# Row indices read in place by the gathers, and an early square root ahead of the norms' squares, in a decoder layer with product-key experts

## The reference, cut to what matters

```python
def peer(x, w_q, sub_keys, u_tab, v_tab):        # 8 heads, 128 keys, top 16, 128*128 experts
    ...
        best, pos = lax.top_k(cand.reshape(TOKEN_BLOCK, PEER_HEADS, PEER_TOPK * PEER_TOPK), PEER_TOPK)
        ids = jnp.take_along_axis(cand_ids.reshape(...), pos, axis=-1)
        g = jax.nn.softmax(best, axis=-1)
        u = u_tab[ids]
        v = v_tab[ids]
        h = jax.nn.gelu(jnp.einsum('td,thkd->thk', xb, u))
        w = (g * h.astype(jnp.float32)).astype(xb.dtype)
        return jnp.einsum('thk,thkd->td', w, v)
x = layer_norm(ALPHA * x + mixed @ w_out[i], ln1_g[i], ln1_b[i])
x = layer_norm(ALPHA * x + peer(x, ...), ln2_g[i], ln2_b[i])
x = x + jax.nn.sigmoid(x @ w_pg + b_pg) * (p[i] @ W_p)
```

## Time and profile before

| | |
|---|---|
| median of 3 runs | 3905.25 us (3902.64 to 3909.58) |
| the profiled execution | 3903.89 us, its span 3902.1 us |
| PE busy | 3808.9 us (98% of the span) |
| PEld (weight loads) busy | 3471.3 us (89%) |
| DVE busy | 2682.2 us (69%) |
| ACT busy | 1403.7 us (36%) |
| POOL busy | 1265.6 us (32%) |
| mean DMA rate | 219 GB/s |
| granted TensorE clock, mean | 0.994 |

### The profile page before, as it was taken

The page is one execution under the profiler, slowest core; times in us unless marked ns, Lnnn a source line. Parts: engine busy times, 40 slices in busy tenths (PEclk is TensorE's granted clock), DMA queues, the critical chain, the costliest instruction groups (busy, mean ns, idle before and its releaser), DMA issues.

```text
span 3902.1 us, 57973 instructions
## 1 busy us (share of the span) xinstructions
PE 3808.9 (98%) x20449; PEld 3471.3 (89%) x20449; DVE 2682.2 (69%) x3814; ACT 1403.7 (36%) x1992; POOL 1265.6 (32%) x620
## 2 busy tenths in 40 slices
PE   8999999999998999999999999989999999999999
PEld 6888888878886889999999999989999999999777
DVE  3555555534413899878878878778888888898642
ACT  4433444441114223446546545222222222222442
POOL 4444444434443447422222222212212211222233
PEclk9999999999999999999999999999999999999999
DMA  4222222224433324698998898978877877787332
GB/s 156 95 97 97 102 94 94 94 99 152 148 121 108 108 89 160 232 367 321 361 373 314 340 378 328 404 294 315 306 288 279 318 289 283 285 311 278 119 105 78
DMA packets 210825, 856.40 MB, mean 219 GB/s; under 512 B 17520, under 2 KB 107824, under 8 KB 119216
## 3 DMA queue, kind: packets, MB, share of 16 engines
q1 hardware_dynamic: 137648, 515.62, 36.6%
q0 software_dynamic: 41600, 302.04, 19.2%
q10 hardware_dynamic: 31488, 37.76, 2.7%
HBM read 788.21 MB, written 67.11 MB: 219 GB/s over the span
## 4 chain that ended last, share of the span: by engine, by line
PE 75%; DVE 9%; DMA 7%; DVEq 3%; ACT 3%; issue 2%; ACTq 1%; SPq 0%
PE bank L631 24%; PE bank L633 23%; PE bank L632 23%; DMA raw<-ws 7%; DVE wlo L1611 2%; PE bank L875 2%; DVEq L1625 2%; DVE yacc L1715 2%; ACT whi L1027 1%; DVE sc L1416 1%; PE bank L674 1%; DVEq L1709 1%; PE bank L693 1%; DVE hot L1600 1%; DVE res L1757 1%
## 5 line engine op out<-in xcount | busy, mean ns | idle before, releaser
L1027 ACT ACTIVATE whi<-raw 128x1024 fp32r<-128x1024 f32 x784 | 820.6, 1057 | 2253.9 <-PE bank L633 1429.2
L631 PE MATMUL bank<-ahi,whi 128*128 128x352 f32 (+1 forms) x3968 | 1434.6, 362 | 32.2 <-DVE alo L1365 7.9
L632 PE MATMUL bank<-alo,whi 128*128 128x352 f32 (+1 forms) x3968 | 1413.8, 356 | 0.0
L633 PE MATMUL bank<-ahi,wlo 128*128 128x352 f32 (+1 forms) x3968 | 1413.6, 356 | 0.0
L594 POOL TENSOR_TENSOR wlo<-raw,whi 128x1024 fp32r<-128x1024 f32 x316 | 792.0, 2510 | 1050.3 <-ACT whi L1027 1021.5
L631 PEld LDWEIGHTS bank<-ahi,whi 128*128 128x128 f32 x3968 | 749.8, 189 | 126.7 <-issue 35.9
L633 PEld LDWEIGHTS bank<-ahi,wlo 128*128 128x128 f32 x3968 | 749.4, 189 | 77.3
L632 PEld LDWEIGHTS bank<-alo,whi 128*128 128x128 f32 x3968 | 749.5, 189 | 72.1 <-issue 0.5
L1611 DVE TENSOR_TENSOR wlo<-raw,whi 128x1024 fp32r<-128x1024 f32 x472 | 574.7, 1223 | 190.6 <-ACT whi L1027 188.3
L631 PE MATMUL bank<-xwhi,whi 128*128 128x384 f32 x2048 | 686.7, 335 | 19.3 <-ACT hst L1226 10.3
L633 PE MATMUL bank<-xwhi,wlo 128*128 128x384 f32 x2048 | 685.7, 335 | 0.0
(11 more groups left out here) (218 smaller groups left out, 2809.8 us busy)
## 6 DMA issues: line engine op xcount, KB each, us to landing
raw<-ws SPq DMA_DIRECT2D x394, 1024.0 KB, 4.9
gelu_spill<-hst ACTq DMA_DIRECT2D x128, 192.0 KB, 3.7
route_spill<-gst SPq DMA_DIRECT2D x24, 1024.0 KB, 14.8
hg<-gelu_spill SPq DMA_DIRECT2D x64, 384.0 KB, 6.7
hg<-route_spill SPq DMA_DIRECT2D x64, 384.0 KB, 7.4
gate_spill<-gout ACTq DMA_DIRECT2D x32, 256.0 KB, 2.1
gl<-gate_spill SPq DMA_DIRECT2D x32, 256.0 KB, 2.7
xin<-xT SPq DMA_DIRECT2D x8, 512.0 KB, 8.6
```

Source lines behind the costliest of these rows:

```text
L631: pe.matmul(ps_out, hi, xh, start=first, stop=False)
L632: pe.matmul(ps_out, hi, xl, start=False, stop=False)
L633: return pe.matmul(ps_out, lo, xh, start=False, stop=last)
L1027: act.activation(whi[:, s], raw[:, s // 2, s % 2], ACT.Copy).then_inc(hi_done, 1)
```

## The change

GpSimd reads each gather's index straight from `idx` or `xg`; `idxs`, `name_rows` and all its calls are gone, with the drains around the copies. The dots and additions themselves increment a new semaphore `rows_used`, for which GpSimd waits before it fills a buffer of the ring again. The first gather of `u_tab` waits for `idx_ok` (now incremented once, with the drain after the picks' transposes are copied) and for `xg_in`, for which VectorE waited before. The first gathers of `v_tab` wait on GpSimd for `blk_done` at `B6`. In `norm_squares` ScalarE first takes the square root of `eps` into one column of `std`.

```diff
-        idxs = small("idxs", [P, RING, 8], U32)
+        rows_used = sem("rows_used")
-            def gather_rows(first, n_rows, table, rows):
-
-                for n in range(n_rows):
-                    s = n % RING
-                    pool.wait_ge(idx_ok, first + n + 1)
+            def gather_u():
+
+                pool.wait_ge(idx_ok, 1)
+                pool.wait_ge(xg_in, 16 * NJ)
+                for n in range(NUP):
+                    if n >= RING:
+                        pool.wait_ge(rows_used, n - RING + 1)
+                    at_col = xg[:, 0, n:n + 1].bitcast(U32) if n < NXP else idx[:, n - NXP:n - NXP + 1]
                     nc.gpsimd.indirect_dma_start(
-                        rows[:, s], None, table,
-                        bass.IndirectOffsetOnAxis(ap=idxs[:, s, 0:1], axis=0)).then_inc(rows_in[s], 16)
+                        urows[:, n % RING], None, u_tab,
+                        bass.IndirectOffsetOnAxis(ap=at_col, axis=0)).then_inc(rows_in[n % RING], 16)
+
+            def gather_v():
+
+                pool.wait_ge(blk_done, B6)
+                for n in range(NP):
+                    if n >= RING:
+                        pool.wait_ge(rows_used, NUP + n - RING + 1)
+                    nc.gpsimd.indirect_dma_start(
+                        vrows[:, n % RING], None, v_tab,
+                        bass.IndirectOffsetOnAxis(ap=idx[:, n:n + 1], axis=0)).then_inc(rows_in[n % RING], 16)
...
             def norm_squares(i, n, src):
+
+                act.activation(std[:, 0:1], eps[:], ACT.Sqrt)
                 for k in range(n):
...
-            dve.drain()
+            dve.drain().then_inc(idx_ok, 1)
...
-            def name_rows(n, s, extra=False):
-
-                src = xg[:, 0, n:n + 1].bitcast(U32) if extra else idx[:, bass.ds(n, 1)]
-                dve.tensor_copy(idxs[:, s, 0:1], src).then_inc(idx_ok, 1)
-
-            def dot(n, m, s, more=True):
+            def dot(n, m, s):
...
                 dve.scalar_tensor_tensor(rows, rows, 1.0, x1n[:, :, TD:T], ALU.mult, ALU.mult,
-                                         accum_out=hd[:, bass.ds(n, 1)])
-                dve.drain()
-                if more:
-                    name_rows(n + RING, s)
+                                         accum_out=hd[:, bass.ds(n, 1)]).then_inc(rows_used, 1)
...
-            dve.wait_ge(xg_in, 16 * NJ)
-            for n in range(RING):
-                name_rows(n, n, extra=True)
             dve.wait_ge(x1e_ok, 5)
...
-                    dve.scalar_tensor_tensor(yacc[:], vrows[:, s], w, yacc[:], ALU.mult, ALU.add)
-                dve.drain()
-                if more:
-                    name_rows(n + RING, s)
+                    dve.scalar_tensor_tensor(yacc[:], vrows[:, s], w, yacc[:], ALU.mult, ALU.add
+                                             ).then_inc(rows_used, 1)
...
             dve.wait_ge(blk_done, B6)
-            for n in range(RING):
-                name_rows(n, n)
             dve.wait_ge(p_in, 16)
```

More of the change, by code:

```diff
@@ L607, in spread_picks @@
                                    ).then_inc(xg_in, 16)
[L609 to L616 removed]
+            def gather_u():
[5 more added lines that the diff above has]
+                    at_col = xg[:, 0, n:n + 1].bitcast(U32) if n < NXP else idx[:, n - NXP:n - NXP + 1]
+                    nc.gpsimd.indirect_dma_start(
+                        urows[:, n % RING], None, u_tab,
[8 more added lines that the diff above has]
+                        bass.IndirectOffsetOnAxis(ap=idx[:, n:n + 1], axis=0)).then_inc(rows_in[n % RING], 16)
             lo_parts(0, DVE_LO)
             spread_picks()
[L620 to L621 removed]
+            gather_u()
+            gather_v()
             pool.wait_ge(lo_done, B7)
@@ L1633, in extra_dot @@
                 dve.scalar_tensor_tensor(rows, rows, 1.0, x1e[:, :, TD:T], ALU.mult, ALU.mult,
-                                         accum_out=hx[:, n:n + 1])
-                dve.drain()
[L1636 to L1639, removed]
+                                         accum_out=hx[:, n:n + 1]).then_inc(rows_used, 1)
                 if n == NXP - 1:
@@ L1687, in _ @@
                 if with_dot:
-                    dot(n - NXP, n // RING, n % RING, more=n + RING < NUP)
+                    dot(n - NXP, n // RING, n % RING)
                     n += 1
@@ L1705, in expert_weights, with add_rows @@
                                   ).then_inc(w_ok, 1)
-            def add_rows(n, m, s, first=False, more=True):
+            def add_rows(n, m, s, first=False):
                 dve.drain()
@@ L1712, in add_rows @@
                 if first:
-                    dve.tensor_scalar(yacc[:], vrows[:, s], w, None, ALU.mult)
+                    dve.tensor_scalar(yacc[:], vrows[:, s], w, None, ALU.mult).then_inc(rows_used, 1)
                 else:
-                    dve.scalar_tensor_tensor(yacc[:], vrows[:, s], w, yacc[:], ALU.mult, ALU.add)
-                dve.drain()
-                if more:
-                    name_rows(n + RING, s)
+                    dve.scalar_tensor_tensor(yacc[:], vrows[:, s], w, yacc[:], ALU.mult, ALU.add
+                                             ).then_inc(rows_used, 1)
             for k in range(8):
@@ L1769, in add_values @@
                     else:
-                        add_rows(8 * g + u, 2 * g + u // RING, u % RING, more=not (last and u >= RING))
+                        add_rows(8 * g + u, 2 * g + u // RING, u % RING)
                     if ahead:
```

## The result

The changed kernel takes 3886.02 us (median of 5 runs, 3882.45 to 3886.93); the kernel before took 3904.87 beside it (5 runs, 3901.25 to 3909.58). The profiled executions' spans are 3902.1 and 3880.7 us.

A forecast was written before the change was run, and what follows sets the result against it. TensorE, with 75% of the chain, was taken as the bound, so only its idle time could shrink. Terms -3.8 - 0.2 + 3.5 - 2.8 + 1.35 = -1.95 us took 3905.25 to 3903.3, range 3893 to 3911.

The forecast's parts named there:

- Part 4: Value stage: without copy and drains after `add_rows`, five back edges shorten by 0.36 us each, a sixth wait by 1.0; -2.8.
- lower bound of -8.9: Value stage: the most that removing copies and drains after additions could give, TensorE's six waits for `res`, 8.9 us.
- Part 1: Routing tiles: without copy and drains after dots, 3.3 us less in looped first halves, 0.5 in second halves; -3.8 us.
- Rival A: Tiles and value stage: VectorE is the bound, so dots and adds count fully where TensorE idles; 3890 us, chance 0.2.
- Part 2: Ahead of the tiles' first `wlo`: four copies go and the wait for `xg_in` moves to GpSimd; -0.2 us.
- Part 3: Before the value stage: four first `v_tab` gathers go 12 us sooner and slow a weight load on the path; +3.5 us.
- promised sign: Before the value stage: early `v_tab` gathers make the weight load on the path land in 12 to 13 us, not 9.19.
- lower bound of 0: Before the value stage: early gathers cost nothing if the load's bytes are all ahead of theirs.
- Rival B: Before the value stage: early gathers halve the load from their issue and delay later loads; 3912 us, chance 0.12.
- Part 5: Three norms: the early square root of `eps` costs 1.45 us in the third, three removed loads give 0.1; +1.35 us.
- rival C: Norms: squares need another table load, 1.28 us more in the third and 0.3 in the second; 3904.9 us, chance 0.08.

The follow-up runs named there:

- 8 later: The kernel before with eight more drains on VectorE ahead of its value loop, copies kept: 3890.69 us, ratio 0.9965.
- v side alone: The kernel before with only the change on the side of `v_tab`; dots and norms as before: 3893.98 us, ratio 0.9982.
- u side alone: The kernel before with only the change on the side of `u_tab` (160 dots without copy and drains): 3880.54 us, ratio 0.9943.

## Why the prediction was wrong

**Part 4 failed at one step, and it was the largest: it took the time at the back edge for fixed.** The prediction had read 7.07 us without work behind `wlo`, called them the cost of jumping back, and only shortened the path by the copy's 0.36. An idle time that nothing in the rows explains was booked as a constant. In truth it hung on where the loop stands in the program, and any edit ahead of the loop that removes or adds instructions moves it. The shift by eight drains shows it: 12.5 us of value stage; the comparison with 1076.1 in place of 1079.6 makes it 9. The term that was worked out is worth nothing: with the loop in a good place, the value stage takes 1067.1 us with copies (8 later) and 1067.5 without (v side alone). TensorE's waits of 8.9 us were the right quantity to look at; I priced what stood beside their cause. The lower bound of -8.9 was nearly the size of the gain, by luck, since it stood for something else.

**Part 1 was right in first halves and failed in second ones.** It had priced 33 dots of the looped tiles at 0.10 us, since `wlo` behind a dot then waits for `whi` alone, and nothing in the unrolled tiles. The looped first halves got shorter by 0.9 us each, 2.7 in all where 3.3 was taken, and the last tile's by nothing. The period of a step with a dot is 4.83 us where it was 4.93, and 4.84 was promised:

```profile
2084.09 1.22 DVE L1626 TENSOR_TENSOR wlo<-raw,whi 128x1024 fp32r<-128x1024 f32 x1 [2.41 <-ACT whi L1040]
...
2088.92 1.23 DVE L1626 TENSOR_TENSOR wlo<-raw,whi 128x1024 fp32r<-128x1024 f32 x1 [0.19 <-ACT whi L1040]
```

The step "in second halves the transfers are full, and a request made 0.3 us earlier moves no byte sooner" is what failed: 0.5 us was taken, the second halves got shorter by 4.4, and their copies put back alone cost 7.7. The queue is full, but the request stands in a loop with the landing of the load before it (two buffers of `raw`), and what a late load costs is paid by the next tile's first one-hots. The trace of the kernel before had the sign: of the 2.4 us that TensorE idles from 2118 to 2185, none lies ahead of 2182, and one wait of 2.8 us for `hot2w` ends the stretch. Rival A had the size: it would be true, the prediction said, "if the tiles get shorter by 2 us each", and they got shorter by 9.5 / 5 = 1.9 each. But its mechanism did not come: `wlo` moved by 0.09 to 0.10 us in its period and no more. "VectorE is the bound" was too coarse; "VectorE is in the loads' loop" is what the traces point to.

**Part 2** (-0.2): the first one-hot matmul starts at 1616.63 before and 1616.66 after, and from 1614.3 to 1617.0 in all sixteen kernels; nothing to see.

**Part 3** (+3.5) was sized wrongly. GpSimd's timeline in the changed kernel has the first gather go out with the last expert block:

```profile
2550.95 1.14 POOL L627 DMA_INDIRECT vrows<-v_tab,idx  x1 [33.91 <-PE bank L646]
```

But the load that was to be slowed down had been issued earlier and landed 1 us behind it; pieces of the changed kernel's chain there:

```profile
2544.32 7.70 DMA raw<-ws
...
2559.36 5.63 SPq L510
```

The promised sign, 12 to 13 us for that load, did not come; the gaps give +0.9. The lower bound of 0 was the better value. Rival B's sign, a gap longer by more than 7 us, did not come.

**Part 5** (+1.35) was right: +1.5 in the third norm and no more. In the first two norms nothing changed, one load stands ahead of the squares and none behind them, so rival C is out as well; in the second norm `std` starts 1.17 us behind the last sum's weight load, where 1.22 was promised.

Together: tiles about -9.5, the back edges about -8 to -12, the third norm +1.5, the gap +0.9, which makes -15 to -19; measured -18.9. Two independent gains, each thought to be small, came together, and one of them owed nothing to what the change is about. The u side alone and the v side alone show it: each alone takes the back edges' loss away.

## What to carry to other kernels

An idle time marked "issue" of several us at a loop's back edge, with packets on the engine's instruction queue in each iteration, is not a constant: count the loop's instructions and where it starts, and move it by a few drains before pricing any edit in it. An edit that changes the number of an engine's instructions ahead of a loop should be compared against a version that changes that number and nothing else. Here a full DMA queue didn't make an engine's latency free, since the request for the next load waits for that engine: ask what the delay does to the lead, and who needs the lead next.

## What the runs showed of the hardware

On VectorE, instructions arrived here in packets of 8192 bytes, one per 128 instructions in straight code. A loop that touched three packets fetched none at its back edge; loops that touched four fetched five packets an iteration. The jump then took 2.8 us to its first instruction (branch 2846.89, move 2849.70) where it took 0.3 without a fetch, and another 5.1 us (to the drain at 2854.76) when that one instruction was the last of its packet. With 25 instructions from the target to the border the second part was hidden. Seven microseconds five times cost TensorE 7 to 9 us of waiting and the stage 8 to 12.5; an iteration of 133.12 us became 134.5 to 137.1, and why it varied so in the kernel before was not found. A table load of the square root's function was followed by squares without a second load, with 0.02 us between the load's end and the activation.
